# Sixteen small copies per tile, split 8 and 8 or 12 and 4 between VectorE and ScalarE

## What is computed

```python
xn = rms_norm(h, norm_in[l])
proj = jnp.einsum('bsd,dn->bsn', xn, w_in[l])
a_q, a_k, a_v, a_g, b_cq, b_ckv, b_kr, b_g = jnp.split(proj, _SPLITS, axis=-1)
q = apply_axial_rope(rms_norm(q, a_q_norm[l]), rope_a)      # 8 heads of 64, k: 2 heads of 64
...
qb = jnp.einsum('bsr,rn->bsn', c_q, w_uq[l])                # 4 heads of 96 from a latent of 384
kvb = jnp.einsum('bsr,rn->bsn', c_kv, w_ukv[l])             # 4 heads of 64 + 128 from a latent of 256
...
y = jnp.concatenate([y_a * jax.nn.silu(a_g), y_b * jax.nn.silu(b_g)], axis=-1)
h = h + jnp.einsum('bsm,md->bsd', y, w_out[l])
```

## Time and profile before

| | us |
|---|---|
| time, median of 3 runs | 1582.37 |
| lowest and highest of them | 1581.68, 1583.48 |
| the profiled execution's own time | 1582.79 |
| its span, first to last instruction | 1581.0 |
| TensorE busy | 1532.8 (97%) |
| VectorE busy | 1303.4 (82%) |
| ScalarE busy | 1236.1 (78%) |
| ScalarE, moves L620, 124 of them in all | 79.1 |
| VectorE, moves L878, 128 of them in all | 45.8 |

### The profile page before, as it was taken

How to read it: one execution, slowest core, us unless ns; L and a number is a source line. 1 busy time by engine, 2 the same in 40 slices (tenths; PEclk the granted TensorE clock), 3 DMA queues, 4 the chain that set the end, 5 groups by cost and what they waited for, 6 DMA issues and landing times.

```text
span 1581.0 us, 37756 instructions
## 1 busy us (share of the span) xinstructions
PE 1532.8 (97%) x13326; PEld 888.3 (56%) x13326; DVE 1303.4 (82%) x1948; ACT 1236.1 (78%) x1671; POOL 589.0 (37%) x506
## 2 busy tenths in 40 slices
PE   7999999999998899999999999999999999999999
PEld 3555555555553465565566566556656655654444
DVE  6886676776888788988998998999899899987764
ACT  8787667667657688888888888888888888877663
POOL 0100000000003465665666666566666656550000
PEclk9999999999999899999999999999999999999999
DMA  9454454453323543243244334325324432536663
GB/s 337 120 127 77 112 116 70 109 110 70 82 64 99 115 98 81 62 103 72 67 106 96 65 73 96 79 62 114 73 69 92 96 79 63 143 101 212 201 198 106
DMA packets 251044, 166.70 MB, mean 105 GB/s; under 512 B 65424, under 2 KB 230800, under 8 KB 250992
## 3 DMA queue, kind: packets, MB, share of 16 engines
q1 hardware_dynamic: 227632, 151.48, 38.5%
q10 hardware_dynamic: 22464, 13.63, 3.1%
q0 software_dynamic: 896, 0.93, 1.0%
HBM read 119.16 MB, written 40.93 MB: 101 GB/s over the span
## 4 chain that ended last, share of the span: by engine, by line
PE 54%; DVE 8%; issue 4%; ACT 1%; DMA 1%; SPq 1%; DVEq 0%; ACTq 0%
PE p_acc L2080 5%; PE p_st L2043 5%; PE p_st L2044 5%; PE p_acc L2084 5%; PE hand_mx L2011 4%; DVE hand_part L1887 4%; PE p_acc L2086 4%; PE p_acc L2085 3%; PE p_st L2046 3%; PE p_st L2047 3%; PE p_st L1499 3%; PE p_st L1502 3%; PE p_st L1500 3%; PE hand_mx L2013 3%; PE p_acc L2081 2%
## 5 line engine op out<-in xcount | busy, mean ns | idle before, releaser
L1789 POOL TENSOR_TENSOR p_pl<-p_p,p_ph 128x512 f16<-128x512 f32 x384 | 507.2, 1327 | 298.7 <-ACT p_ph L1828 238.0
L1887 DVE TENSOR_REDUCE hand_part<-hand_mx 128x2 f32<-128x1024 f32 x373 | 454.8, 1219 | 72.6 <-PE hand_mx L2011 54.7
L1819 ACT ACTIVATE p_p<-p_st 128x1024 f32<-128x1024 f32 x384 | 391.0, 1019 | 95.0 <-PE p_st L2051 51.9
L1195 PE MATMUL p_ring<-p_w_hi,p_xT 128*128 128x512 f16 (+3 forms) x1536 | 389.2, 338 | 7.7 <-DVE p_w_lo L903 5.1
L1828 ACT ACTIVATE p_ph<-p_p 128x1024 f16<-128x1024 f32 x334 | 353.1, 1057 | 18.3
L1915 DVE TENSOR_TENSOR p_pl<-p_p,p_ph 128x512 f16<-128x512 f32 x384 | 326.5, 851 | 8.3 <-ACT p_ph L1828 7.6
L1195 PE MATMUL p_ring<-p_w_lo,p_xT 128*128 128x512 f16 (+3 forms) x768 | 259.7, 338 | 0.0
L1195 PEld LDWEIGHTS p_ring<-p_w_hi,p_xT 128*128 128x128 f16 x1536 | 150.7, 98 | 127.2 <-DVE p_xT L861 5.7
L2080 PE MATMUL p_acc<-p_vas,p_ph 128*128 128x129 f16 x2048 | 208.8, 222 | 0.0
L2043 PE MATMUL p_st<-early 128*128 128x512 f16 x512 | 194.8, 380 | 9.0 <-ACT p_p L1819 8.8
L2080 PEld LDWEIGHTS p_acc<-p_vas,p_ph 128*128 128x128 f16 x2048 | 181.3, 97 | 37.0 <-issue 17.8
(11 more groups left out here) (194 smaller groups left out, 2368.1 us busy)
## 6 DMA issues: line engine op xcount, KB each, us to landing
p_vbs<-scratch_vb SPq DMA_DIRECT2D x16, 1028.0 KB, 6.4
p_xin<-in_x SPq DMA_DIRECT2D x16, 512.0 KB, 8.4
p_xcol<-in_x_cols SPq DMA_DIRECT2D x16, 512.0 KB, 7.4
scratch_g<-p_g SPq DMA_DIRECT2D x16, 512.0 KB, 3.4
p_kb<-scratch_kb SPq DMA_DIRECT2D x32, 256.0 KB, 5.5
p_vas<-in_x SPq DMA_DIRECT2D x16, 512.0 KB, 4.0
out<-p_ph SPq DMA_DIRECT2D x15, 512.0 KB, 2.8
out_gt<-scratch_g ACTq DMA_DIRECT2D x13, 512.0 KB, 3.5
```

The costliest lines, as they stand in the source:

```text
L1195: last = pe.matmul(ring_t[:, 0:w], a, b, start=(k == 0 and m == 0), stop=(k == len(steps) - 1 and m == len(terms) - 1))
L1789: pool.tensor_tensor(pl[:, s % NP, 1, :], p32[:, s % N32, QB:], ph[:, s % NP, 1, :], ALU.subtract).then_inc(s_lop, 1)
L1819: act.activation(p32[:, s % N32, :], st[:, s % 2, :, :].rearrange("p a b -> p (a b)"), ACT.Exp, scale=scale).then_inc(s_exp, 1)
L1887: dve.tensor_reduce(part[:, e // MPAIRS % 3, 2 * c:2 * c + 2], mx[:, :, :], AX, ALU.max).then_inc(s_red, 1)
```

## The change

The default share of `z_move` becomes quadrant 3 alone on ScalarE and quadrants 0, 1 and 2 on VectorE. It holds for tiles 0 to 12, so 52 long moves change engine. Tile 13 had this split by an explicit argument, which is dropped; tiles 14 and 15 stay as they are.

```diff
-            def z_move(t, h, pr, c0=0, c1=NCH, quadrants=(2, 3)):
+            def z_move(t, h, pr, c0=0, c1=NCH, quadrants=(3,)):
 
                 act.wait_ge(s_zh, t + 1)
...
-                    z_move(T13, 1, PAIRS - 2, quadrants=(3,))
+                    z_move(T13, 1, PAIRS - 2)
...
-            def z_move(t, h, pr, c0=0, c1=NCH, quadrants=(0, 1)):
+            def z_move(t, h, pr, c0=0, c1=NCH, quadrants=(0, 1, 2)):
 
                 dve.wait_ge(s_zl, t + 1)
...
-                    z_move(T13, 1, PAIRS - 2, quadrants=(0, 1, 2))
+                    z_move(T13, 1, PAIRS - 2)
```

## The result

The changed kernel takes 1586.07 us (median of 14 runs, 1582.42 to 1587.56), the kernel before beside it 1581.54 us (14 runs). The ratio is 1.0028, 95% interval 1.0021 to 1.0036: **4.4 us slower**, 3.3 to 5.7. The forecast was 3.07 us slower, which on the 1582.37 us of the first three runs gave 1585.4 us.

A forecast was written before the change was run, and what follows sets the result against it. TensorE was taken as the bound, full from about 110 us to the loop's end, so only the loop entry counts: 0.67 us delay plus 2.4 us clock fall, 3.07 us on 1582.37, gives 1585.4 us; range 1582.1 to 1586.9.

The forecast's parts named there:

- Loop tiles at nothing: In the loop: VectorE's extra 1.53 us fits its 7.16 us idle time, so eleven or so tiles cost nothing.
- Price of the moves: Per tile, four long moves add about 1.53 us on VectorE and take 3.62 us off ScalarE.
- the reciprocal at 91.29: Tile 2's `latent_rstd` on VectorE follows the longer moves, starting at 91.29 us instead of 89.76.
- ScalarE's waits: At loop entry, TensorE's waits for ScalarE's copies of `cq` (1.31 us) and `ag` (0.69 us) go.
- 0.67 us of place: At loop entry, `bg` of tile 2 starts at 102.56 us instead of 101.89, 0.67 us later.
- The clock falls at tile 2: TensorE's 3.36 us stall before tile 2's transposes drops the clock to 1.2 GHz, costing 2.4 us; chance 0.66.
- Tile 15's stall of 2.65 us put at nothing: Before 470.93 us, TensorE's 2.65 us stall showed no clock fall behind it; the sum has no term for it.
- The sum: Whole kernel: 0.67 us of delay plus 2.4 us for the clock, 3.07 us slower, 1585.4 us.
- Same or slower: Whole kernel: 3.07 us lies just inside the 0.2% (3.2 us) bound; same 0.66, slower 0.32, faster 0.02.
- The clock stays up: Rival at tile 2's stall: no clock fall, only 0.67 us lost, 1583.0 us; chance 0.24.
- ScalarE gates: Rival at tile 2: `latent_rstd` does not move, both ScalarE waits go, 2.17 us gained, 1580.2 us; chance 0.05.
- Late row statistics: Rival in the loop: VectorE's longer copies hold back GpSimd's small DMAs, 18 us slower, 1601 us; chance 0.02.

The follow-up runs named there:

- e6: e1 with three more unused reductions of 1408 columns on VectorE behind its moves in each loop tile; 1583.96 us, ratio 1.0008.
- e7: e1 with five more unused reductions of 1408 columns on VectorE behind its moves in each loop tile; 1596.97 us, ratio 1.0095.
- e4: Changed kernel, TensorE's first loop pair written out, 16 unused matmuls filling tile 2's stall before the transposes; 1584.64 us, ratio 1.0011.
- e1: New split (12 copies VectorE, 4 ScalarE) in tiles 1 to 12 only, tile 0 as in the kernel before; 1582.71 us, ratio 0.9992.
- e2: New split at tile 0 alone, all other tiles as in the kernel before; 1586.78 us, ratio 1.0024.
- e5: Changed kernel with TensorE's first loop pair written out, without extra matmuls (control for e4); 1586.39 us, ratio 1.0022.
- e11: The same changed kernel run once more, on a chip shared with other runs; 1586.61 us, ratio 1.0021.
- e3: New split in tiles 1 to 12, at tile 0 ten copies on VectorE and six on ScalarE; 1584.10 us, ratio 1.0009.
- e8: e1 with ScalarE's first output-weight piece at step 18 of the attention stage's first half instead of 11; 1574.38 us, ratio 0.9952.
- e12: e8 plus four repeated 512-column matmuls in tile 12, moving all that follows on TensorE; 1575.75 us, ratio 0.9956.
- e10: Kernel before with only ScalarE's first output-weight piece at step 18 instead of 11, all moves 8 and 8; 1574.84 us, ratio 0.9947.
- e9: e8 plus eleven unused 512-column matmuls in TensorE's stall at tile 15; 1575.71 us, ratio 0.9949.

## Why the prediction was right and where it was not

- **Loop tiles at nothing: right.** 330.00 of 330 us after, VectorE's idle time 5.63 us (7.16 less 1.53); e6 and e7 bracket the point from which it would cost.
- **Price of the moves, the reciprocal at 91.29, ScalarE's waits: right.** 4.52 and 1.90 us, 91.39, and ScalarE's copies of `cq` 3.52 us earlier. The wait of TensorE became 3.53 us where 3.36 was worked out.
- **0.67 us of place: right,** 0.62 in e4, with e1 giving the 0.85 of the `ag` wait by itself.
- **The clock falls at tile 2: right, its price too high.** I took 2.4 us from the kernel's start, bounds 0 and 3.0. With 0.67 taken off, the profiles with the stall of about 3.5 us show 2.18 (after), 1.63 (e2, e5) and 1.64 (e11), e3 1.64. The 2.4 came from the durations of the kernel's first matmuls alone: the profile's granted clock reads 1.00 there from 10 us on (before), and it was a start, not a stall. `bg` came at 104.83 where "near 105" stood.
- **Tile 15's stall of 2.65 us put at nothing: wrong.** This is the term that the sum lacks. The earlier trace rows showed no fall behind it, in one execution of one kernel, and I took the size of the stall as the reason. The clock fell at the same stall in after, e1, e2, e3, e5, e7, e8, e11 and e12, and not in e4, e6 and e10. Each fall costs some 1.5 us: from these transposes to the first score matmuls it is 498.74 - 473.88 = 24.86 us in after and 494.24 - 470.93 = 23.31 before. The same reading stood behind the expectation of e3, whose stall of 2.75 us did bring a fall; in e9 even one of 2.15 us did.
- **The sum.** By the profile of after: 0.67 + 2.18 at tile 2, 1.55 behind tile 15, less 1.3 around the long stall, gives 3.1 us for a difference of the spans of 3.2. The runs give 4.4 (3.3 to 5.7), 3.3 (1.9 to 4.8, e11) and, with the moves of the changed kernel and TensorE written out, 3.5 (1.9 to 5.2, e5). That the 3.1 meets the forecast of 3.07 is in part luck: 2.4 was more than the clock cost at tile 2, and neither the 1.55 lost at tile 15 nor the 1.3 that came back was in the forecast. After and e11 are the same kernel, and their runs' mean clocks are 0.9949 (14 runs) and 0.9958 (12 runs); 0.0009 of 1584 us is 1.4 us, about what their differences from before are apart. So the clock's spread between executions would account for 4.4 against 3.3 us. That 4.4 against 3.07 is this and nothing else is argued; the intervals leave about 1 us open.
- **Same or slower.** I held the sum to be just inside what can be told from no change, and gave "same" twice the chance of "slower". With terms this firm (no rival that gives anything back survived e1 to e5), and a second place that was not counted, the sum lay at the bound or above, and by that bound of 0.2% the runs say slower (1.0021 to 1.0036). A sum at the bound is worth near even chances, and any uncounted loss falls on one side of it.
- **The rivals.** The clock stays up: not in any profile with the stall. ScalarE gates: no, its wait for the reciprocal grew to 5.58 us. Late row statistics: TensorE does not wait anywhere in the loop. The load that was issued at 155.06 us before is issued at 158.04 in after, 2.98 us later like all else there, and so in the midst of VectorE's copies (154.79 to 159.34) instead of behind them; it landed 3.7 us after its issue, before 3.6. Neither its issue nor its landing was held back by the copies to an extent that matters.

The Trainium skill ("TensorE: Matmul & The Clock Gate", Part 1) says that only activity releases the full rate, and that the point of the change varies by about half a microsecond from run to run. e4 agrees with the first: activity whose result is unused kept it. The second is said of the rise under steady work, and the rises here agree: they come 98.3 - 92.66 = 5.6 us behind the first transposes in after, 96.8 - 91.75 = 5.1 in e11 and 97.1 - 92.42 = 4.7 in e5. The falls are spread wider: in after the clock fell 1.2 us ahead of the first transposes (91.4, they start at 92.66), in e11, the same kernel, 1.7 us behind them (the window 92 to 94 has 0.86, so near 93.4; they start at 91.75). That is 2.9 us apart, and it is why the price was 2.18 us in one and 1.64 in the other: half of the slow time of the matmuls that wait for nothing, 93.72 to 98.3 in after (2.3), 93.4 to 96.8 in e11 (1.7).

## What to carry to other kernels

Moving work to another engine is free only where that engine has idle time ahead of its next hand-over; count it at each place, the entry into a loop above all: here four copies at tile 0 cost what e2 shows, while 48 in the loop cost nothing that could be measured. Price a new stall of TensorE as its idle time plus the slow matmuls behind it: here 0.62 us and 1.6 to 2.2. And follow the longest stall of the page back to its cause before moving small work about: a weight converted seven steps later gave 8 us.

## What the runs showed of the chip

- **Stalls of 2.15 to 2.75 us can bring the clock down to 1.2 GHz, and need not.** The same 2.65 us at the same place did in e12 (470.94) and did not before (470.93); 2.15 us at 493.43 did in e9 only.
- **A fall removed can turn up elsewhere.** With tile 15's stall filled, the one profile shows falls at the next stall and from 510 to 516 instead, and nothing was gained: e9 1575.71 us (ratio 0.9949), e8 1574.38 (0.9952).
- **The mean granted clock of each run is a measure of its own.** At 1575 us, 0.001 is 1.6 us of the span, about the size of one such fall. Five runs of e8 at 0.999 and five of e10 at 1.000 tell more than one profile of each, but the means of before (35 runs) and of e1 (11 runs) do not bear out that the split makes the difference (0.9972 and 0.9970).
